# A 32-byte pad behind the small persistent tiles of a two-block transformer kernel

## What is computed

```python
def first_block(x, ...):                       # cut to the products
    h = rms_norm(x, pre_mix_norm)
    proj = h @ w_in                            # 2048 x 5656
    ...                                        # differential attention (8 heads), NSA attention (8 heads)
    x = x + rms_norm(mix @ w_out, post_mix_norm)       # 2048 x 2048
    h = rms_norm(x, pre_ffn_norm)
    u = causal_dwconv(h @ w_up, conv_w, conv_b)        # 2048 x 11264
    gate, up = split(u)
    y = (gelu(gate) * up) @ w_down                     # 5632 x 2048
    return x + rms_norm(y, post_ffn_norm)

def second_block(x, ...):
    h = rmsnorm(x, norm_pre_mix)
    m = hgrn2_mixer(h, w_in, w_out, ...)               # 2048 x 10240, a gated scan both ways, 2048 x 2048
    x = x + rmsnorm(m, norm_post_mix)
    h = rmsnorm(x, norm_pre_ffn)
    return x + rmsnorm(conv_ffn(h, ...), norm_post_ffn)   # 2048 x 11264 and 5632 x 2048, silu
```

## The kernel before

| tile | start | over a multiple of 64 |
|---|---|---|
| raw, whi, wlo, x | 16512, 32896, 49280, 65664 | 0 |
| ident | 82048 | 0 |
| rstd, prs, prime, psq | 85632, 85664, 85696, 85728 | 0, 32, 0, 32 |
| ybuf, utok0, ptok, mix2 (first byte of the region) | 85856 | 32 |
| hhi, hlo | 102240, 147296 | 32 |
| qkT, pst, toep | 130912, 130912, 136608 | 32 |
| wghl | 181600 | 32 |
| cfold, gate, posT, w2, hidT | 185792, 185920, 186112, 186368, 188416 | 0 |
| pc, pcs, nmx, psm, cof, dsq, drs | 191872 and on | 0 |
| qd0, kd0, kd1, at, vt | 155488, 163680, 167776, 171872, 181088 | 32 |
| ahi, alo | 194400, 210784 | 32 |
| prb0, pts0, blkhl, csum | 198496, 202592, 207712, 223072 | 32 |

## Time and profile before

### The profile page before, as it was taken

The page is one execution under the profiler, slowest core; times in us unless marked ns, Lnnn a source line. Parts: engine busy times, 40 slices in busy tenths (PEclk is TensorE's granted clock), DMA queues, the critical chain, the costliest instruction groups (busy, mean ns, idle before and its releaser), DMA issues.

```text
span 2733.4 us, 37125 instructions
## 1 busy us (share of the span) xinstructions
PE 2634.4 (96%) x13482; PEld 2112.3 (77%) x13482; DVE 1620.8 (59%) x1856; ACT 1357.8 (50%) x1785; POOL 194.8 (7%) x92
## 2 busy tenths in 40 slices
PE   8799788999999999999999999999999999999998
PEld 6688656878888887888787878878788888887886
DVE  4344663556666666544548587695566666665444
ACT  4344553455555555333454544545555555554342
POOL 1000000001112121100000000000011112121000
PEclk9899865999999999999999999999999999999999
DMA  8866310555666665655565555554566666555554
GB/s 200 234 190 185 114 55 29 180 155 177 183 184 178 183 181 165 211 189 186 161 190 166 169 170 155 155 163 162 154 192 177 177 183 184 178 183 194 190 185 138
DMA packets 242450, 465.01 MB, mean 170 GB/s; under 512 B 14344, under 2 KB 23345, under 8 KB 241841
## 3 DMA queue, kind: packets, MB, share of 16 engines
q1 hardware_dynamic: 240001, 453.44, 54.5%
q0 software_dynamic: 2240, 10.21, 1.8%
q10 hardware_dynamic: 112, 0.03, 0.0%
HBM read 458.40 MB, written 5.23 MB: 170 GB/s over the span
## 4 chain that ended last, share of the span: by engine, by line
PE 94%; DVE 2%; ACT 2%; DMA 1%; issue 1%; SPq 0%; DVEq 0%; ACTq 0%
PE acc L219 29%; PE acc L220 29%; PE acc L221 28%; DMA raw<-in_w_in_dram 1%; PE tp L462 1%; PE tp L960 1%; PE tp L265 1%; PE tp L1296 1%; PE acc L924 1%; DVE wlo L206 1%; PE tp L1324 1%; PE tp L941 1%; PE tp L1275 0%; PE tp L962 0%; DVE x L432 0%
## 5 line engine op out<-in xcount | busy, mean ns | idle before, releaser
L206 DVE TENSOR_TENSOR wlo<-raw,whi 128x1024 fp32r<-128x1024 f32 x856 | 1148.6, 1353 | 940.4 <-ACT whi L201 938.3
L201 ACT ACTIVATE whi<-raw 128x1024 fp32r<-128x1024 f32 x856 | 904.1, 1060 | 1102.0 <-PE acc L221 1039.5
L219 PE MATMUL acc<-whi,ahi 128*128 128x512 f32 x2656 | 1062.0, 400 | 21.4 <-DVE wlo L206 14.5
L220 PE MATMUL acc<-wlo,ahi 128*128 128x512 f32 x2656 | 1051.1, 396 | 0.0
L221 PE MATMUL acc<-whi,alo 128*128 128x512 f32 x2656 | 1050.9, 396 | 0.0
L219 PEld LDWEIGHTS acc<-whi,ahi 128*128 128x128 f32 x2656 | 499.8, 188 | 142.0 <-DVE wlo L206 22.7
L221 PEld LDWEIGHTS acc<-whi,alo 128*128 128x128 f32 x2656 | 499.0, 188 | 122.3
L220 PEld LDWEIGHTS acc<-wlo,ahi 128*128 128x128 f32 x2656 | 499.9, 188 | 116.5
L219 PE MATMUL acc<-whi,hhi 128*128 128x512 f32 x704 | 278.2, 395 | 0.0
L220 PE MATMUL acc<-wlo,hhi 128*128 128x512 f32 x704 | 278.1, 395 | 0.0
L221 PE MATMUL acc<-whi,hlo 128*128 128x512 f32 x704 | 278.1, 395 | 0.0
(11 more groups left out here) (208 smaller groups left out, 1304.7 us busy)
## 6 DMA issues: line engine op xcount, KB each, us to landing
raw<-in_w_up_dram SPq DMA_DIRECT2D x176, 512.0 KB, 3.8
raw<-in_ffn_w_in_dram SPq DMA_DIRECT2D x176, 512.0 KB, 4.1
raw<-in_hgrn_w_in_dram SPq DMA_DIRECT2D x160, 512.0 KB, 3.7
raw<-in_w_in_dram SPq DMA_DIRECT2D x88, 512.0 KB, 3.7
raw<-in_w_down_dram SPq DMA_DIRECT2D x88, 512.0 KB, 4.3
raw<-in_ffn_w_out_dram SPq DMA_DIRECT2D x88, 512.0 KB, 4.3
raw<-in_w_out_dram SPq DMA_DIRECT2D x32, 512.0 KB, 4.3
raw<-in_hgrn_w_out_dram SPq DMA_DIRECT2D x32, 512.0 KB, 4.0
```

Source lines behind the costliest of these rows:

```text
L201: act.activation(whi[:, s, :], raw[:, s, :], ACT.Copy).then_inc(hi_done, 1)
L206: dve.tensor_tensor(wlo[:, s, :], raw[:, s, :], whi[:, s, :].bitcast(F32), ALU.subtract).then_inc(lo_done, 1)
L219: pe.matmul(out[:, t, :], xh, whi[:, s, c], start=(kt == 0), stop=False)
L220: pe.matmul(out[:, t, :], xh, wlo[:, s, c], start=False, stop=False)
```

## The change

One tile of 8 float32 values a partition (32 bytes) is allocated behind the last persistent tile. Nothing reads or writes it.

```diff
         prime = sb("prime", [P, 1])
         psq = sb("psq", [P, 4, NT, NG])
+        sb("pad64", [P, 8])
```

## The result

The median went from 2729.81 us (4 runs of the kernel before, the three named above among them) to **2667.89 us** (4 runs, 2667.44 to 2669.03). The ratio is 0.9773, 95% interval 0.9757 to 0.9790: 61.9 us less. I had forecast no change, 2729.6 us, with 0.14 for faster.

A forecast was written before the change was run, and what follows sets the result against it. PE was taken to bound the kernel: 10,080 products at 0.2333 us, 2352 us of the 2733.4 us span. Four terms, 0 + 0 + 0 + 0, left the median at 2729.6 us, range 2718 to 2741.

The forecast's parts named there:

- terms 2 to 4: Transposes and small products; VectorE, ScalarE and GpSimd; DMAs at the start: 0 each, the last with 1.4 us either way.
- term 1: Loads of stationary tiles for the 10,080 products: alignment changes 0, with 10 us either way at 1 ns a load.
- Rival A: Product loads: aligned tiles save a ninth 64-byte line, 138 us, giving 2591 us (mild form 6 us, 2723 us); chance 0.14.
- Rival B: Products: both operands starting on a line meet in SBUF, 73 us more, 2803 us; chance 0.09 with other losses.
- theory 2c: From e5_micro2's own forecast: product spacing is a rhythm the stream locks into, with short cycles and other means, some perhaps lower.

The follow-up runs named there:

- e1_micro: Matmuls alone, places of stationary (sta) and moving (mov) operand over a multiple of 64 varied; 512 columns: 226.7 ns with both 0, 233.2 with sta 32.
- e2_front: Pad ahead of raw instead, against the kernel before: moving operand 32 bytes over a multiple of 64, stationary tiles at one; 2732.59 us, ratio 1.0011.
- e3_both: Both pads, against the kernel before: moving operand and stationary tiles all 32 bytes over a multiple of 64; 2669.31 us, ratio 0.9778.
- e5_micro2: Matmuls alone in the kernel's order, either or both operands' offsets moved in steps of 32 bytes: 226.7 ns at difference 0, 233.3 at 32.

## Why the prediction was wrong

**What held.** PE bounds the kernel, 10,080 products are what can move, 20.0 ns of each are beyond streaming, no other engine's busy time moved by 0.2%, the loads keep their 188 ns and the transposes their 0.87 us, terms 2 to 4 come to nothing that the traces show.

**The step that failed** is in term 1: "the surplus halves when the moving operand halves, and hardly cares for the stationary one [...]: it belongs to the moving side", and so I put the term at 0. It was 6.3 ns a product. I drew a line through two points of a jagged function. e1_micro has the rest of it. At unequal places (`sta` 32, `mov` 0) the surplus over N/2.4 is 11.6 ns for 256 columns, 13.3 for 384 and 20.0 for 512; at equal places it is 13.3 for all three. At equal places it is thus the same for these three lengths (at 128 columns it is not), and at 512 columns an unequal placing adds 6.7 ns, half of it again. It belongs to neither operand alone. The row at half clock, with nothing beyond, was no evidence either: it reads 426 to 427 ns at equal places too.

**The second step that failed** was to let other kinds of matmul price this one. `x` against `utok` is an honest pair, also modulo 256 (`x` stands as `ident` does, `utok` 32 bytes off), and it does show nothing. But a transpose is no float32r product of 512 columns. In the compression product the step l = 2 that I took for the equal place stands 64 bytes off `whi`, and the other three of the earlier trace rows stand 32, 48 and 80 off: none was equal. Besides, it has 256 moving columns, and e1_micro shows that there the placing costs nothing or the other way. The sign that I had named for this came: the products' spacing fell and that of `utok`'s transposes did not. I took the rounding of those rows, 1 ns, as the bound of term 1. It was only the error of the reading. The bound of the carry-over was the unexplained 20.0 ns, 201.6 us, and the measured 6.3 ns lies well within it.

**Rival A** had the sign by a wrong mechanism: no ninth line is paid, since e2_front reads eight lines a tile and is slow, and e3_both reads nine and is fast. The sign that I had given for it, a spacing that falls towards 220 while the compression's and the gate's stay, came in the main (226.7 ns), so it could not tell this rival from another. **Rival B** looked at the right quantity, the places of the two operands to each other, with the sign turned round: of the places in steps of 32 bytes the equal ones are the cheap ones.

The Trainium skill would have led the same way ("TensorE: Matmul & The Clock Gate", Part 2: What happens when you issue a matmul): loading the next weights, it says, does not take SBUF read bandwidth from the running matmul, for TensorE has two independent read ports. By that rule the places could not matter to each other. e2_front and e3_both differ by 63 us in that alone, so here the measurement decides against what I draw from the rule; whether bandwidth is what is lost, no run shows. Nor do the 16-byte cachelines that the Trainium skill gives in "SBUF — State Buffer" (Door 1: The DMA port swizzle) explain it: all places of 0 to 224 in steps of 32 start such a line.

What stays open is the cause inside the chip. The runs show that the spacing follows sta minus mov within 256 bytes as long as both stand at multiples of 32, and both at 16 (231.1 ns) shows that this is not the whole rule. Whether two reads meet in some part of SBUF, or something else has that period, no run here tells.

## What to carry to other kernels

A surplus per instruction that is not explained bounds the gain of a forecast, whatever pairs of rows of another shape say; here it was 201.6 us and I had put it at 10. Where float32r products of 512 columns bound a kernel, put the stationary and the moving tiles at the same place within 256 bytes, each at a multiple of 32, and check the distance between starts, not the durations; a stream of matmuls alone foretold the whole kernel to 3 us. And test a change's own description too: "multiples of 64" hit the right place by luck, and a pad of 96 bytes, as true to it, gives nothing.

## What the runs showed that I had not expected

The spacing locks into a rhythm. e5_micro2 with both operands at 128, starts of the first products after a line at another place (start us, us):

```profile
819.52 0.39 PE L105 MATMUL acc<-mhi,shi 128*128 128x512 f32 x1
819.75 0.39 PE L105 MATMUL acc<-mlo,shi 128*128 128x512 f32 x1
819.97 0.39 PE L105 MATMUL acc<-mhi,slo 128*128 128x512 f32 x1
820.20 0.40 PE L105 MATMUL acc<-mhi,shi 128*128 128x512 f32 x1
820.44 0.39 PE L105 MATMUL acc<-mlo,shi 128*128 128x512 f32 x1
820.67 0.40 PE L105 MATMUL acc<-mhi,slo 128*128 128x512 f32 x1
820.90 0.39 PE L105 MATMUL acc<-mhi,shi 128*128 128x512 f32 x1
```

In ns the distances are 230, 224, 231, 236, 228, 233, 231, 226, and from there 227, 227, 226 to the end of the line. With `mov` 64 and `sta` 0 the line settles into 229, 232, 226 instead, and now and then 231 for 232. That is theory 2c, as far as its short cycles go; a placing that is faster did not turn up. Single distances of 224 occur, but no placing tried holds them: the best steady value seen is 226.7 ns, 544 cycles of 2.4 GHz, and the most frequent other one 233.3 ns, 560 cycles.
